# One written order of events per engine for the first layer of a two-layer decoder trunk

## The chip, the cores and the metric

The kernel runs on one core of a Trainium2 chip. The metric is device time in microseconds (us) of one execution, as the median of several. TensorE is called PE in the profile (its weight loads PEld), VectorE DVE, ScalarE ACT, GpSimd POOL, SyncE SP.

## The reference

Input x is 1024 tokens by 1024 channels, float32. Two layers are computed; after each, `x = LayerNorm(4^0.25 * x + mixer(x))`.

Layer 0 is a gated DeltaNet with 8 heads of width 128. A projection gives q, k, v and a gate z (32 column tiles of 128) and two small gate rows; q, k and v pass a causal convolution of 4 taps and SiLU; q and k are normalised. Per head and per chunk of tokens: decay and score matrices, a unit lower triangular inverse, and then a recurrence over the chunks:

```
v_new = u_n - w_n @ state
o     = q_n @ state + qk_n @ v_new
state = state * exp(gl_n) + kd_n.T @ v_new
```

The output of each head is RMS-normalised, multiplied by SiLU(z), and projected. Layer 1 is sliding-window attention; nothing of it is touched here.

## The kernel before

**Numbers and tiles.** Every float32 operand of a large product is split in a high and a low part, and a product is three matmuls (high-high, high-low, low-high) of 128 x 128 x 512. A projection group `g` is one column tile (128 channels) times one half of the tokens (512): 8 depth slices x 3 = 24 matmuls, `project` at L654. There are 64 groups after two for the gate rows: 6 for each head (q, q, k, k, v, v; heads 0 to 7), then 16 for z. One phase is six groups, 144 matmuls. Chunks of 128 tokens are used, so each head has 8.

**What hangs on a group.** After the last matmul of a group ACT copies the PSUM bank out (`evacuate`, L1099 and L1100), DVE does three taps of the convolution (`piece` 0 to 2, L1401), ACT a tanh (`gate_tanh`, L1106), DVE the last product (`piece` 3, L1418). The groups alternate between two PSUM banks. Weights of the next tile are fetched by DMA on ACT's queue and split on ACT (`high`, L1047) and DVE (`low`, L1325).

**What hangs on a head.** In this order:
- T, `token_major`: twice, 4 chunks at a time, PE transposes k, v and q of the head into banks 7, 5, 6 (L723); ACT copies v (L1113), DVE makes `k_dec` (L1483), ACT squares and sums k and q (L1122), each square waiting for the sum before it.
- M, `scores` on PE (L738, L739) for 8 chunks, with ACT's `exp` of the decay (L1190) and DVE's `matrices` (L1441, L1443), in banks 5, 6, 7 in turn.
- The inverse of the 32 x 32 diagonal blocks: SP sends the blocks out to HBM and back in another layout (L501, L506), POOL does 30 steps of two instructions (L609, L612), SP sends them back into `xT` (L509, L516). There is one `xT`, so SP waits for the last solve of the head before.
- X and L: DVE transposes blocks (L1513 to L1516), then four levels of small matmuls (`level`, L760 to L773) with copies on ACT and DVE between them complete the inverse of each chunk.
- Scan: for each chunk A (`with_state`, L784, L787), B (`solve`, L799) and C (`update`, L807, L809) on PE. Between A and B lies DVE's `resid` (L1531), between B and C ACT's `v_new` (L1208), between C and the next A DVE's `state` (L1540) and output sum (L1547); ACT scales `q_state` (L1203) and squares the output (L1129). A waits for the state and for the output sum of the chunk before.
- Output: OF, OS, OT: root of the sums, scaling (L1497), transposes back (`transpose_out`, L817) and copies into `tok` (L1184).

**What sets the order.** PE, ACT and DVE execute their instructions in program order. The order is written out by `plan(p, lag)`: for each phase `p` it gives every event a place, counted in matmuls from the start of the phase (constants `AT_...`, as a share of the phase), adds a lag per kind for ACT and DVE (`LAG_SCALAR`, `LAG_VECTOR`), and sorts. The lists of the phases are then run one after another, so all pieces of the last group of a phase stand ahead of everything of the next phase. Phases 8 and 9 have 10 and 6 groups (z), phase 10 has none: it holds the output of head 7 beside the first two steps of the output projection (`out_pair`, L826). SP and POOL have fixed orders of their own.

Of the kernel before, what the change touches and what calls it, by code (L numbers as in the profile page):

```python
# [100 lines left out]
def plan(p, lag):


    if p < GH:
# [1 line left out]
    elif p == GH:
        groups = list(range(QKV_GROUPS, QKV_GROUPS + GATE_SPLIT))
    elif p == GH + 1:
        groups = list(range(QKV_GROUPS + GATE_SPLIT, 2 * TILES))
    else:  # L110
        groups = []
    last = 2 * TILES - 2
    events = []
    for i, g in enumerate(groups):
        t0 = GROUP * i
        for q in range(0, GROUP, STEP):
            events.append((t0 + q, 0, ("mm", g, q)))
        end = t0 + GROUP - 0.5
        events.append((end, 1, ("end", g, 0)))
        if g % 2 == 0 and g // 2 + 1 < TILES:  # L120
            events.append((t0 + 6.6, 1, ("weights", g // 2 + 1, 0)))
            if g // 2 + 2 < TILES:
                events.append((t0 + 15.9, 1, ("fetch", g // 2 + 2, 0)))
        if g % 2 == 0 and g // 2 + 1 < TILES:
            events.append((t0 + 6.8, 1, ("low", g // 2 + 1, 0)))
        for k in range(CONV_K if g < QKV_GROUPS else 2):
            if g < last:
                events.append((end + 0.58 + k * 6.95, 2, ("piece", g, k)))
            elif k == 0:
                events.append((end + 0.2, 2, ("piece", g, k)))  # L130
    span = GROUP * max(len(groups), 1)
    slots = []
    if 0 <= p - 3 < GH or 0 <= p - 2 < GH:
        slots += [(AT_ROOTS, ("OF", 0))]
    if 0 <= p - 3 < GH:
        slots += [(AT_SCALE, ("OS", 0)), (AT_OUT, ("OT", 0))]
    if p == GH + 2:
        slots += [(0.02 + 0.02 * k, ("W", k)) for k in range(2)]
        for k in range(3, EARLY[0]):
            slots += [(0.14 + 0.02 * k, ("WW", k)), (0.145 + 0.02 * k, ("WO", k))]  # L140
    if p == GH + 1:
        events += [(t0 + 5.0 + 3 * k, 3, ("WO", k, 0)) for k in range(3)]
        events += [(t0 - 16.0 + 9 * k, 3, ("WW", k, 0)) for k in range(3)]
    if 0 <= p - 2 < GH:
        slots += [(AT_VALUES, ("VS", 0))]
    if 0 <= p - 1 < GH:
        slots += [(AT_TOKEN[i], ("T", i)) for i in range(2)]
        slots += [(AT_MATRIX + AT_MATRIX_STEP * c, ("M", c)) for c in range(NT + 1)]
    for r in (p - 3, p - 2):
        if 0 <= r < GH:  # L150
            blocks, inverse, scan, step = (AT_BLOCKS, AT_INVERSE, AT_SCAN, AT_SCAN_STEP) if r < GH - 1 else \
                                          (LAST_BLOCKS, LAST_INVERSE, LAST_SCAN, LAST_SCAN_STEP)
# [1627 lines left out]
```

## Time and profile before

| what | us |
|---|---|
| median of 3 runs | 1170.51 |
| the three runs | 1169.4, 1170.51, 2981.0 |
| the profiled execution | 1165.01 |
| its span, first to last instruction | 1163.0 |
| PE busy in it | 1067.3 (92%) |
| DVE, ACT, POOL busy | 720.4, 502.8, 322.1 |
| mean granted TensorE clock | 0.973 |

An instruction is shown with its line in the kernel before. "Busy" is the union of instruction times; matmuls overlap, so a busy PE can still hold short gaps. First group of layer 0's projection after the start-up: about 67 us; its last matmul starts at 652.71 us. The output projection follows, and from about 880 us layer 1's attention.

### The profile page before, as it was taken

What the parts mean: (1) busy time and instruction counts of PE and PEld (TensorE: products, weight loads), DVE (VectorE), ACT (ScalarE), POOL (GpSimd) and SP (SyncE); (2) the same over time, 40 slices, a digit from 0 to 9 for tenths busy, and PEclk for the clock granted to TensorE, in tenths of its full rate; (3) what the DMA queues carried; (4) which work ended last, traced back from release to release, by engine and by line L of the source; (5) the groups of instructions that cost most, each with busy time, mean ns of one, the idle gap of its engine ahead of it and who ended that gap; (6) DMA issues with size and microseconds to landing.
All of it is one profiled execution on the core that took longest, in us unless ns stands there. A gap on an engine that the chain in (4) does not pass through costs nothing. (4 is left out here: it accounts for less than half of the span.)

```text
span 1163.0 us, 17699 instructions
## 1 busy us (share of the span) xinstructions
PE 1067.3 (92%) x6325; PEld 847.9 (73%) x6325; DVE 720.4 (62%) x1650; ACT 502.8 (43%) x1386; POOL 322.1 (28%) x517
## 2 busy tenths in 40 slices
PE   7989678888979899898999999999997999999996
PEld 6768556666767676666877788888885777777885
DVE  4557446566556566664545877763437787787865
ACT  4453625546464554645343701120215656657100
POOL 1005857192855829393560000000000000000000
PEclk9999869999989999999999999999999999999998
DMA  5112111102012011201121241220200000012211
GB/s 185 56 37 64 37 37 46 46 21 62 28 28 64 24 50 38 55 19 46 47 61 40 91 145 45 65 82 1 64 19 1 28 29 20 19 49 94 94 55 55
DMA packets 74510, 59.50 MB, mean 51 GB/s; under 512 B 23148, under 2 KB 65196, under 8 KB 74424
## 3 DMA queue, kind: packets, MB, share of 16 engines
q1 hardware_dynamic: 40104, 41.53, 11.6%
q10 hardware_dynamic: 34320, 16.84, 5.6%
q8 instruction: 51, 0.84, 0.3%
q14 instruction: 35, 0.29, 0.1%
HBM read 52.04 MB, written 6.32 MB: 50 GB/s over the span
## 5 line engine op out<-in xcount | busy, mean ns | idle before, releaser
L654 PE MATMUL ps<-act_hi,w_hi 128*128 128x512 f32 x528 | 238.8, 452 | 0.0
L654 PE MATMUL ps<-act_hi,w_lo 128*128 128x512 f32 x528 | 211.6, 401 | 0.0
L654 PE MATMUL ps<-act_lo,w_hi 128*128 128x512 f32 x528 | 210.2, 398 | 0.0
L609 POOL TENSOR_TENSOR rank<-tok 32x30 f32<-32x30 f32 (+14 forms) x240 | 153.1, 638 | 48.6 <-DMA tok<-blocks_in 30.4
L612 POOL TENSOR_TENSOR tok<-tok,rank 32x30 f32<-32x30 f32 (+14 forms) x240 | 151.1, 629 | 18.8
L1401 DVE SCALAR_TENSOR_TENSOR tok<-xs,convw,tok 128x512 f32<-128x512 f32 x144 | 118.6, 824 | 32.3 <-ACT xs L1100 30.6
L654 PEld LDWEIGHTS ps<-act_hi,w_lo 128*128 128x128 f32 x528 | 101.4, 192 | 23.3
L654 PEld LDWEIGHTS ps<-act_hi,w_hi 128*128 128x128 f32 x528 | 102.9, 195 | 11.1
L654 PEld LDWEIGHTS ps<-act_lo,w_hi 128*128 128x128 f32 x528 | 103.0, 195 | 9.5
L826 PE MATMUL ps<-wo_hi,act_hi 128*128 128x512 f32 x256 | 100.5, 393 | 0.2 <-DVE wo_lo L1459 0.2
L826 PE MATMUL ps<-wo_hi,act_lo 128*128 128x512 f32 x256 | 99.7, 390 | 0.0
L826 PE MATMUL ps<-wo_lo,act_hi 128*128 128x512 f32 x256 | 99.6, 389 | 0.0
L597 POOL TENSOR_SCALAR_AFFINE_SELECT decay<-decay 128x1024 f32<-128x1024 f32 x8 | 8.7, 1094 | 217.5 <-DMA decay<-gc_rows 217.5
L1235 ACT ACTIVATE mv<-mv 128x1 f32<-128x1 f32 x16 | 3.2, 203 | 130.5 <-DVE mv L1608 130.5
L1203 ACT ACTIVATE q_state<-ps,sc_exp 128x128 f32<-128x128 f32 x56 | 20.6, 368 | 88.2 <-PE ps L787 88.1
L826 PEld LDWEIGHTS ps<-wo_hi,act_hi 128*128 128x128 f32 x256 | 48.1, 188 | 11.0 <-issue 1.0
L826 PEld LDWEIGHTS ps<-wo_hi,act_lo 128*128 128x128 f32 x256 | 48.0, 188 | 10.2
L826 PEld LDWEIGHTS ps<-wo_lo,act_hi 128*128 128x128 f32 x256 | 48.1, 188 | 9.8
L1325 DVE TENSOR_TENSOR w_lo<-w_raw,w_hi 128x1024 fp32r<-128x1024 f32 x33 | 43.6, 1322 | 15.2 <-ACT w_hi L1047 14.9
L981 PE MATMUL ps<-act_hi,z_hi 128*128 128x512 f32 x128 | 52.1, 407 | 0.1
L1106 ACT ACTIVATE th<-tok 128x512 f32<-128x512 f32 x48 | 30.1, 627 | 50.9 <-DVE tok L1401 50.8
L981 PE MATMUL ps<-act_lo,z_hi 128*128 128x512 f32 x128 | 51.7, 404 | 0.0
(235 smaller groups left out, 2292.4 us busy)
## 6 DMA issues: line engine op xcount, KB each, us to landing
w_raw<-in_a_w_in ACTq DMA_DIRECT2D x32, 512.0 KB, 4.2
tok<-in_x SPq DMA_DIRECT2D x8, 512.0 KB, 7.2
decay<-gc_rows SPq DMA_DIRECT2D x8, 512.0 KB, 4.3
xres<-in_x SPq DMA_DIRECT2D x8, 512.0 KB, 3.7
ws_raw<-in_b_w_in SPq DMA_DIRECT2D x16, 256.0 KB, 2.7
z_raw<-in_b_w_in SPq DMA_DIRECT2D x8, 512.0 KB, 3.8
out<-yr SPq DMA_DIRECT2D x8, 512.0 KB, 2.6
wo_raw<-in_a_w_out SPq DMA_DIRECT2D x6, 512.0 KB, 4.2
```

What stands on the lines that cost most here:

```text
L597: pool.affine_select(out=decay[:, :, :], in_=decay[:, :, :], compare_op=ALU.is_ge, fill=NEG, base=0, pattern=[[0, NT], [1, P]], channel_mu ...
L609: inner.next(pool.tensor_tensor(part, blocks[:, 0:m, m:m + 1].broadcast_to([32, m, w]), blocks[:, m:m + 1, m + 1:32].broadcast_to([32, m, ...
L612: inner.next(pool.tensor_tensor(blocks[:, 0:m, m + 1:32], blocks[:, 0:m, m + 1:32], part, ALU.add))
L654: mm = pe.matmul(ps[:, g % 2, :], lhs[:, k, :], rhs[:, k, HALF * b:HALF * (b + 1)], start=(i == 0), stop=(i == GROUP - 1))
L826: mm = pe.matmul(ps[:, OUT_BANKS[t] + half, :], lhs[:, k, t * P:(t + 1) * P], rhs[:, HALF * half:HALF * (half + 1)], start=(k == 0 and j = ...
L981: mm = pe.matmul(ps[:, GATE_BANK, :], lhs[:, k, :], rhs[:, k, HALF * b:HALF * (b + 1)], start=(i == 0), stop=(i == GROUP - 1))
L1106: act.activation(th[:, :], conv[g % 2], ACT.Tanh).then_inc(s_th, 1)
L1203: act.activation(q_state[:, :], ps[:, 3, 0:P], ACT.Copy, scale=sc["exp"][:, r, a:a + 1])\
L1235: act.activation(mv[:, t % 2, 3:4], mv[:, t % 2, 2:3], ACT.Sqrt).then_inc(s["sqrt"], 1)
L1325: dve.tensor_tensor(w_lo[w % 2][:, :, :], w_raw[:, :, :], w_hi[w % 2][:, :, :].bitcast(F32), ALU.subtract).then_inc(s_wlo, 1)
L1401: ins = dve.scalar_tensor_tensor(conv[b], xs[:, b, k:k + HALF], convw[:, k, tile:tile + 1], conv[b], ALU.mult, ALU.add)
```

## The change

It replaces the per-phase lists by one list per engine over the whole layer.

- `plan(at, lag)` makes one sorted list for each of PE, ACT and DVE. Every event of head h stands at `SPAN * (h + place + late)`, with SPAN = 144 matmuls. Places are tables of their own per engine (`AT_PE`, `AT_ACT`, `AT_DVE`), and each head has a shift for its first half (`LATE_TURN`: T, M) and for its second (`LATE_SCAN`: X, L, scan, output). From its first transposes to its output a head takes some 2.7 phases, from its first group 3.3.
- T is split in three: TQ (q, place 0.60, banks 7 and 5), TK (k, 0.95, banks 6 and 7) and TV (v, 1.27, banks 6 and 7, after the scores). The squares are written over their own PSUM source and don't wait for each other. The eight `exp` of a head's decay are one block on ACT (D).
- PSUM: `resid`'s product stays in bank 2, `q_state`'s goes to bank 4, B and C's output to bank 3, levels to 5 and 6, output transposes to 7 and 5. A no longer waits for the output sum.
- Two `xT` buffers: SP waits for the solves of the head before the last. `xr` and `uT` get room outside `o_tok`.
- In ACT's scan the copies QS, VN and the squares SO are placed one by one; in DVE's RE, ST, OA.
- `EARLY` goes from (5, 1) to (3, 1): the splits of output weights 3 and 4 are no longer written into the plan, and the output of head 7 comes before the end of the projection. The output projection then begins at k = 0 in `out_stage`.

The counts of matmuls, transposes, copies and DMAs stay; POOL clears four more slices at the start.

```
+SPAN = 6 * GROUP
+AT_PE = {"TQ": [0.6028], "TK": [0.9491],
+          "M": [0.9757, 0.9963, 1.017, 1.037, 1.058, 1.078, 1.099, 1.119],
+          "TV": [1.274], "OT": [3.261], "L": [2.332, 2.351, 2.388, 2.409],
+          "S": [2.415, 2.437, 2.458, 2.482, ...
+AT_DVE = {... "X": [2.276], "M": [0.9901, ..., 1.134], ...
+LATE_TURN = [-0.0781, 0.0, 0.1933, 0.15, 0.15, 0.1097, 0.0501, 0.05]
+LATE_SCAN = [0.204, 0.15, 0.15, 0.1, 0.0576, 0.05, 0.0, 0.1466]
+LAG_ACT = {"end": -0.528, "piece": 6.271, "weights": 0.867, "fetch": -0.08}
+LAG_DVE = {"piece": 2.595, "low": 4.624}
-    if p < GH:
-        groups = list(range(6 * p, 6 * p + 6))
...
+    for g in range(2 * TILES):
+        t0 = GROUP * g
...
+    for h in range(-1, GH):
+        for kind, places in at.items():
+            for i, place in enumerate(places):
...
+                late = 0.0 if kind == "TQ" else LATE_TURN[h] if kind in TURN_KINDS else LATE_SCAN[max(h, 0)]
+                name, c = STEPS[i] if kind == "S" else (kind, i)
+                events.append((SPAN * (h + place + late), 3, (name, h, c)))
     events.sort(key=lambda e: (e[0] + lag.get(e[2][0], 0.0), e[1]))
...
-                if h:
-                    sp.wait_ge(s_y, NT * h)
+                if h >= 2:
+                    sp.wait_ge(s_y, NT * (h - 1))
...
             def scores(h, c):
                 if c == 0:
-                    pe.wait_ge(s_tev, 2 * h + 2)
-                    pe.wait_ge(s_sk, NT * (h + 1))
+                    pe.wait_ge(s_sq, NT * (h + 1))
+                elif c == 1:
+                    pe.wait_ge(s_kd, 2 * h + 1)
+                    pe.wait_ge(s_sk, NT * h + 4)
+                elif c == 2:
+                    pe.wait_ge(s_kd, 2 * h + 2)
+                    pe.wait_ge(s_sk, NT * (h + 1))
...
                 pe.wait_ge(s_state, 7 * h + c)
-                pe.wait_ge(s_o, NT * h + c)
                 pe.matmul(ps[:, 2, 0:P], kT[h % 3][:, cut], state[:, :], start=True, stop=True).then_inc(s_ks, 1)
-                if 7 * h + c - 1 > 0:
-                    pe.wait_ge(s_oq, 7 * h + c - 1)
-                pe.matmul(ps[:, 3, 0:P], qT[h % 3][:, cut], state[:, :], start=True, stop=True).then_inc(s_qs, 1)
+                pe.matmul(ps[:, 4, P:2 * P], qT[h % 3][:, cut], state[:, :], start=True, stop=True).then_inc(s_qs, 1)
...
-            for p, events in enumerate(PLANS):
-                for kind, a, b in events:
+            for kind, a, b in PE_PLAN:
...
+            def sums(h, bank, out_sum, ready, done):
+                for i in range(2):
+                    act.wait_ge(ready, 2 * h + i + 1)
+                    for c in range(4 * i, 4 * i + 4):
+                        cut = ps[:, bank[i], (c - 4 * i) * P:(c - 4 * i + 1) * P]
+                        act.activation(cut, cut, ACT.Square, accum_out=sc[out_sum][:, h, c:c + 1]).then_inc(done, 1)
```

## Rows read from the trace of the kernel before

**Rows 1.** The page: each engine's busy time, granted clock in 40 slices.

```profile
PE 1067.3 (92%) x6325; PEld 847.9 (73%) x6325; DVE 720.4 (62%) x1650; ACT 502.8 (43%) x1386; POOL 322.1 (28%) x517
...
PEclk9999869999989999999999999999999999999998
```

**Rows 2.** By stretch: its us; busy PE, PEld, DVE, ACT, POOL; clock; DMA share, GB/s.

```profile
67.00:118.80 51.80, 47.71 (x243) 39.45 (x241) 31.72 (x56) 26.75 (x72) 18.62 (x25) 1.00 0.20 50
118.80:202.70 83.90, 64.13 (x396) 49.67 (x394) 44.33 (x89) 36.85 (x110) 60.92 (x100) 0.84 0.15 39
202.70:268.80 66.10, 58.02 (x396) 44.39 (x394) 40.54 (x86) 35.56 (x108) 38.00 (x58) 0.97 0.14 37
268.80:335.40 66.60, 58.80 (x395) 45.98 (x394) 41.80 (x86) 35.62 (x108) 40.09 (x63) 0.95 0.15 40
335.40:401.90 66.50, 59.35 (x396) 45.96 (x394) 40.73 (x86) 35.72 (x108) 40.17 (x63) 0.95 0.17 41
...
468.10:538.30 70.20, 62.37 (x423) 48.24 (x421) 42.82 (x88) 37.57 (x108) 42.59 (x72) 1.00 0.17 41
538.30:652.90 114.60, 108.21 (x744) 85.39 (x743) 60.04 (x125) 48.45 (x139) 33.60 (x61) 1.00 0.19 52
```

**Rows 3.** PE's waits within 335.4 to 401.9 us (total us, times, longest).

```profile
PE ps L807 <- ACT v_new L1208: 2.3, 1, 2.3
PE ps L738 <- ACT sq_junk L1122: 1.8, 1, 1.8
PE ps L723 <- ACT sq_junk L1122: 1.4, 2, 1.0
PE ps L784 <- DVE o_tok L1547: 0.7, 2, 0.5
PE ps L770 <- DVE o_tok L1522: 0.5, 1, 0.5
PE ps L817 <- DVE o_tok L1497: 0.4, 1, 0.4
```

**Rows 4.** Two of PE's waits over the whole run.

```profile
PE ps L723 <- ACT sq_junk L1122: 15.8, 16, 4.2
...
PE ps L760 <- DVE o_tok L1516: 12.9, 5, 10.5
```

**Rows 5.** The timeline at the end of one phase (start, duration).

```profile
385.26 2.87 DVE L1401 SCALAR_TENSOR_TENSOR tok<-xs,convw,tok 128x512 f32<-128x512 f32 x3 [0.65 <-ACT xs L1100]
...
388.16 0.63 ACT L1106 ACTIVATE th<-tok 128x512 f32<-128x512 f32 x1 [2.39 <-DVE tok L1401]
...
389.10 0.49 PE L807 MATMUL ps<-v_new,k_dec 128*128 128x128 f32 x2 [2.32 <-ACT v_new L1208]
```

**Rows 6.** The timeline of the inverse of head 0, and the start of head 1's.

```profile
91.95 0.28 DVE L1443 TENSOR_TENSOR aT<-ps,decay 128x128 f32<-128x128 f32 x1
...
99.43 0.24 POOL L609 TENSOR_TENSOR rank<-tok 32x30 f32<-32x30 f32 x1
...
144.73 0.14 POOL L615 MEMSET tok<- 32x32 f32 x1
...
151.22 0.44 DVE L1516 STREAM_TRANSPOSE o_tok<-xT 32x256 f32<-32x256 f32 x1
...
156.24 0.24 POOL L609 TENSOR_TENSOR rank<-tok 32x30 f32<-32x30 f32 x1
```

**Rows 7.** Busy time during the inverses of heads 3 and 7, columns as in rows 2.

```profile
294.20:337.70 43.50, 38.76 (x213) 29.92 (x210) 26.98 (x46) 22.02 (x67) 38.87 (x60) 0.96 0.09 25
564.70:602.80 38.10, 37.70 (x218) 31.18 (x217) 16.43 (x33) 12.58 (x34) 33.44 (x60) 1.00 0.11 28
```

**Rows 8.** The timeline of two projection matmuls in a row.

```profile
652.02 0.40 PE L654 MATMUL ps<-act_hi,w_lo 128*128 128x512 f32 x1
...
652.25 0.40 PE L654 MATMUL ps<-act_hi,w_hi 128*128 128x512 f32 x1
```

**Rows 9.** ACT's squares in the groups by line: busy us, mean ns of one.

```profile
L1122 ACT ACTIVATE sq_junk<-ps 128x128 f32<-128x128 f32 x128 | 35.2, 277 | 9.3 <-DVE k_dec L1483 4.6
```

More of the change, by code:

```diff
@@ L93, in slices_before, with plan @@
     return range(WR, SLICES) if n == refill else ()
-LAG_SCALAR = {"WO": 1.5, "WW": 0.0, "OT": 2.0, "end": 1.7, "piece": 5.5, "A": 1.6, "B": 0.3, "M": 3.0, "T": 0.6, "L": 6.3}
-LAG_VECTOR = {"WO": 5.0, "WW": 4.0, "piece": 0.9, "A": 0.1, "C": 0, "M": 0.8, "T": 1.9, "L": 7.5}
-def plan(p, lag):
-    if p < GH:
-        groups = list(range(6 * p, 6 * p + 6))
[L106 to L112, printed above, removed]
+def plan(at, lag):
     events = []
-    for i, g in enumerate(groups):
-        t0 = GROUP * i
+    for g in range(2 * TILES):
+        t0 = GROUP * g
         for q in range(0, GROUP, STEP):
@@ L121, in plan @@
             events.append((t0 + 6.6, 1, ("weights", g // 2 + 1, 0)))
+            events.append((t0 + 6.8, 1, ("low", g // 2 + 1, 0)))
             if g // 2 + 2 < TILES:
                 events.append((t0 + 15.9, 1, ("fetch", g // 2 + 2, 0)))
-        if g % 2 == 0 and g // 2 + 1 < TILES:
-            events.append((t0 + 6.8, 1, ("low", g // 2 + 1, 0)))
         for k in range(CONV_K if g < QKV_GROUPS else 2):
[L127 to L152, printed above, removed]
-            items = [(blocks, ("X", 0))] + [(inverse + AT_INVERSE_STEP * i, ("L", i)) for i in range(4)]
-            items += [(scan + step * (3 * c + i), ("ABC"[i], c)) for c in range(NT) for i in range(3)]
-            shift = p - 2 - r
-            slots += [(at - shift, (n, c, r)) for at, (n, c) in items if 0 <= at - shift < 1]
@@ L157, in plan @@
-    for at, item in slots:
-        events.append((at * span, 3, (item + (0,))[:3]))
-    events.sort(key=lambda e: (e[0] + lag.get(e[2][0], 0.0), e[1]))
-    out = [e[2] for e in events]
-    if p == GH + 2:
-        out += [("piece", last, 1), ("piece", last + 1, 1)]
-    return out
-PLANS, SCALAR_PLANS, VECTOR_PLANS = ([plan(p, lag) for p in range(GH + 3)] for lag in ({}, LAG_SCALAR, LAG_VECTOR))
+            events.append((end + 0.58 + k * 6.95, 2, ("piece", g, k)))
+    total = 2 * TILES * GROUP
@@ L169 @@
+    events.sort(key=lambda e: (e[0] + lag.get(e[2][0], 0.0), e[1]))
+    return [e[2] for e in events]
+PE_PLAN, ACT_PLAN, DVE_PLAN = plan(AT_PE, {}), plan(AT_ACT, LAG_ACT), plan(AT_DVE, LAG_DVE)
 class Link:
@@ L808, in update @@
                       .then_inc(s_su, 1)
-                pe.matmul(ps[:, 2, P:2 * P], aT[h % 2][:, c, :], v_new[:, :], start=True, stop=True)\
+                pe.matmul(ps[:, 3, P:2 * P], aT[h % 2][:, c, :], v_new[:, :], start=True, stop=True)\
                   .then_inc(s_av, 1)
@@ L913, in out_stage @@
                 before = (None, None, None, 0, 1, 3, 4, 5)
-                for k in range((2, 0)[i], NK):
+                for k in range(NK):
                     out_pair(i, k)
```

495 lines of the change are left out of this document (256 added, 239 removed), and 20 rows, old and new, of tables (AT_ACT, AT_DVE).

## The prediction

> **What bounds the kernel now.** I read the page first. PE is busy 92% of the span, and no other compute engine is above 62% [rows 1]. So the end is set by PE's stream, and time can only come out of it in two ways: fewer matmuls, which this change doesn't bring, or fewer gaps. The slices show where the clock is below its full 2.4 GHz: all but one or two of the lower digits lie in the first half, in layer 0 [rows 1].
>
> Then the busy times by stretch, cut from one head's transposes to the next's [rows 2]. Four stretches between 202.7 and 468.1 us are alike (66.1, 66.6, 66.5 and 66.2 us; the last is not shown). In the third PE is busy 59.35 of 66.50 us, 7.15 idle, at a mean clock of 0.95. A mean of 0.95 between the two levels 1.0 and 0.5 is a tenth of the stretch at 1.2 GHz, 6.6 us; work in it takes twice as long, so at most 3.3 us are lost, and I take half of that, 1.7, since idle time falls in these pieces too. The stretch 118.8 to 202.7 is the bad one: 19.8 us idle, clock 0.84, so 27 us at 1.2 GHz; without the idle 10.5 us some 16 us of work, half of it lost: 8 us. Before it, 4.1 us idle; after 468.1, 7.8 and then 6.4 [rows 2]. Together from 67 to 652.9 us: idle 4.1 + 19.8 + 8.1 + 7.8 + 7.2 + 7.3 + 7.8 + 6.4 = 68.5 us (7.3 is the stretch not shown), clock 8 + 4 x 1.7 = 15. That 83 us is all a new order could give.
>
> Third, what PE waits for in an ordinary stretch [rows 3]: 2.3 for `v_new`, 1.8 and 1.4 for the squares of k and q, 0.7 for the output sum, 0.5 and 0.4 for levels and output scaling. The list sums to 7.1, which is the idle time.
>
> **The change part by part.** The matmuls, transposes and copies stay the same in number, so each term is a wait.
>
> *The phase boundary, 2.3 us.* The row on the timeline is telling: DVE runs three taps in one go, 385.26 to 388.13, ACT's tanh waits 2.39 for them, and `v_new` stands behind the tanh, so PE waits 2.32 [rows 5]. These taps belong to the last group of a phase, and only because the lists are run phase by phase do they stand ahead of the remaining scan steps. One list per engine puts one tap between two scan steps. The wait goes to 0; taps and tanh are late next; they have 20 matmuls of 0.23 us [rows 8], 4.6 us, for 2.87 + 0.63 us of work.
>
> *Transposes and scores, 3.2 us (1.8 + 1.4).* Now k, v and q go through the banks twice, and PE waits each time until ACT has squared both k and q, 8 squares at 277 ns [rows 9] and their reads; q's now come 0.35 phase earlier, v's after the scores. What is left between TK and the third score is one set of eight squares of k, against two score pairs and 9 to 12 matmuls (some 3 us). But the eight `exp` are a block on ACT, behind it comes the tanh, and DVE's `piece` 3 waits for that ahead of the third pair of matrices, which frees the bank of the sixth score. I bound what remains by 0 and by today's 3.2, and take the middle, 1.6: gain 1.6.
>
> *Own banks, 0.7 us.* A waits for the state alone. DVE's output sum is the instruction behind it, so I take 0.5, between 0 and 0.7.
>
> *Levels and output scaling, 0.9 us.* Level 2 gets 5.4 instead of 2.8 matmuls of distance, OT stands 14 matmuls behind OS. Gain 0.7, between 0 and 0.9.
>
> *Clock, 1.7 us.* The low pieces follow the waits of 2 us and more; with the largest gone I take all of the 1.7, between 0 and 3.3.
>
> An ordinary stretch thus gives 2.3 + 1.6 + 0.5 + 0.7 + 1.7 = 6.8 us, and 66.5 becomes about 59.7. Five of them, 202.7 to 538.3: 34 us.
>
> *Head 0 and 1.* PE waits 10.5 us for head 0's inverse, and up to 4.2 for one set of transposes [rows 4]. Head 0's last score moves from place 1 + 0.2837 + 7 x 0.0233 = 1.447 to 1.119 - 0.078 = 1.041, 58 matmuls or 13.4 us earlier, while its X stays at 2.48 (2 + 0.4843; now 2.276 + 0.204). So the 10.5 go. Of the rest of that stretch (9.3 idle, 8 clock) I take 2.3 for its boundary, 4 at the transposes and all of the clock: 10.5 + 2.3 + 4 + 8 = 25. The stretch before: 2 of its 4.1. The last, 538.3 to 652.9: 2 of 6.4, since it has only one head's scores.
>
> *`EARLY`.* The end of the projection loses the output of head 7 from its edge, but the splits of weights 3 and 4 come later. ACT and DVE are free there; PE has three steps of 12 matmuls (2.8 us each) in hand. I take a loss of 1, between 0 and 3.
>
> *What an order by table costs.* Several hundred events get new neighbours in three queues. No row prices an order that hasn't run. The nearest are the small waits of the present order, 0.5 + 0.4 = 0.9 us a head [rows 3]; I take nearly twice that in each of 8 heads, 13 us, between 0 and 30 (half of the 7.1 of [rows 3], 8 times).
>
> Sum: 34 + 25 + 2 + 2 - 1 - 13 = 49 us. The profiled execution took 1165.0 us, so 1116; the median of the runs stands 5.5 us above it, and I carry that over: 1170.5 - 49 = 1121.
>
> **Does the inverse allow it?** Head 0's chain took 59.0 us from the last matrices (92.23) to the last block transpose, 45.3 of them on POOL; and POOL began the next 11.5 us after it ended [rows 6]. In an ordinary stretch the inverse takes 43.5 [rows 7], so POOL can turn a head around in 55.0 us, below the 59.7 I forecast. The tables leave 1.05 to 1.10 phases (151 to 158 matmuls) between the last matrices and X for heads 2 to 6: at 59.7 us for 144 they are 62.6 to 65.5 us, 3.6 to 6.5 more than 59.0. The second `xT` takes the solves out of it.
>
> POOL is slower beside a busy DVE: 43.5 us with DVE at 26.98 / 43.5 = 62%, 38.1 with 43% [rows 7]. DVE's 41 us a stretch [rows 2] in 59.7 would be 69%, and the same slope (5.4 us for 19 points) gives 45.5 us, a turnaround of 57.0: still below.
>
> The Trainium skill, page "SBUF — State Buffer", section "Who interferes with whom", says that a DVE instruction with two SBUF inputs and a GpSimd instruction that reads SBUF take turns, the later one blocked for the whole instruction. By that rule the inverse lengthens as the taps crowd in, and it speaks against this change; the trace agrees in direction (38.1 against 43.5 us).
>
> **The rivals.**
>
> *POOL becomes the bound (chance 0.20).* If the inverse takes 50 to 54 us in the denser stretches, a head costs 61.5 to 65.5 us and X, which stands in DVE's one queue, holds up taps and state behind it. For: the slope above, and the longest inverse of 45.3. Against: 50 needs more than twice that slope. At 63.5 us a stretch gives 3 instead of 6.8: 19 less over five, and some of the start goes too (5), so a gain of 25: 1146, with 1136 to 1160 around it.
>
> *The whole wait list goes (0.12).* Transposes without waits, and no new ones: 49 + 13 + 5 x 1.6 = 70; 1100.
>
> *Scan steps miss each other (0.09), the slower side.* A, B and C stand three matmuls (0.7 us) and the small ones apart, and between them lies a hop through DVE or ACT. If a tap (1.0 us, a third of 2.87 [rows 5]) or a split of weights stands ahead of `resid`, `v_new` or `state` in most steps, each of the 56 steps with a state loses 1 us or more; at 0.9 us per step (50 us) the gain is gone, at 1.3 (73 us) the time is 1195. For: `v_new` shows today what one wrong neighbour costs, 2.3 us. Against: the scan's pitch, 10.1 matmuls against 10.3, hardly changes.
>
> *The order isn't what made PE wait (0.08).* If DVE simply arrives late whatever the list, the waits move: about 1162.
>
> **How the numbers follow.** The forecast, 1121, has 0.51, with its own range 1106 to 1136 from the bounds of its terms. A difference of 2% (23 us) is about what a measurement can tell here from none. Faster by more: all of the forecast (0.51) and the full gain (0.12), and of the POOL case the better half and a little of the rest: 0.75. Within 2%: the rest of the POOL case and most of the last: 0.16. Slower: 0.09. The range goes from 1098 to 1158; it leaves out about 0.05 below and 0.13 above.
>
> **What would show it.** In the profile after: PE waits for `v_new` of 2 us and more are gone at the ends of phases; no wait of PE on the first level of head 0 above 2 us; stretches of 144 matmuls with all parts take 58 to 61 us, at clock 0.97 or better; PE's last projection matmul starts near 603 us. The step on POOL is wrong if inverses last over 48 us, or if DVE's X waits for the `xT` DMA. The forecast is wrong if PE idles over 4 us per head in A, B and C together.

## The result, and the profile after

The changed kernel takes 1090.53 us (median of 4 runs, 1087.56 to 1097.81), the kernel before 1171.95 beside it (median of 4, 1170.51 without the run of 2981.0 us); the ratio, without that run, is 0.932, with a 95% interval of 0.926 to 0.938. Forecast were 1121 us and a range of 1098 to 1158: the sign was right, the size was not, and the time lies below the range. The profiled execution took 1097.81 us, against 1165.01.

The page of the kernel after: busy times, granted clock, and the taps of the convolution, whose last columns are DVE's idle time ahead of them and what ended it.

```profile
PE 1043.7 (95%) x6325; PEld 847.0 (77%) x6325; DVE 725.1 (66%) x1650; ACT 497.4 (45%) x1388; POOL 332.4 (30%) x521
...
PEclk9999979999999999989999999999999999999999
...
L1409 DVE SCALAR_TENSOR_TENSOR tok<-xs,convw,tok 128x512 f32<-128x512 f32 x144 | 121.9, 847 | 9.8 <-ACT xs L1109 8.3
```

The same work by DVE and ACT, and PE's 6325 matmuls in 67 us less span [rows 1]. In the row of the taps the idle time behind ACT's copy is 8.3 us. In the page before it is 30.6, and the prediction gave this row no price:

```profile
L1401 DVE SCALAR_TENSOR_TENSOR tok<-xs,convw,tok 128x512 f32<-128x512 f32 x144 | 118.6, 824 | 32.3 <-ACT xs L1100 30.6
```

Where the time came from, by phases of 144 projection matmuls (from the starts of the matmuls in the two traces). Of the kernel before, and then of the one after, phases 3 to 7, five ordinary ones in a row:

```profile
186.40:251.10 64.70, 56.74 (x398) 43.01 (x396) 40.22 (x86) 35.62 (x108) 31.90 (x54) 1.00 0.16 42
251.10:317.80 66.70, 58.97 (x397) 46.04 (x396) 41.14 (x86) 35.66 (x107) 40.18 (x63) 0.95 0.15 40
...
450.40:516.50 66.10, 57.90 (x398) 44.46 (x396) 41.96 (x86) 35.52 (x107) 42.16 (x66) 0.97 0.16 41
sum 330.10, PE 291.76 PEld 225.44 DVE 204.88 ACT 178.11 POOL 192.98; mean PE 58.35 PEld 45.09 DVE 40.98 ACT 35.62 POOL 38.60
```

```profile
172.80:230.90 58.10, 55.17 (x403) 45.25 (x403) 42.57 (x87) 35.72 (x112) 39.37 (x62) 1.00 0.19 47
...
341.80:400.40 58.60, 56.65 (x410) 45.83 (x409) 42.67 (x89) 35.28 (x113) 43.36 (x65) 1.00 0.18 46
...
sum 284.70, PE 274.97 PEld 224.76 DVE 209.97 ACT 175.53 POOL 203.82; mean PE 54.99 PEld 44.95 DVE 41.99 ACT 35.11 POOL 40.76
```

330.1 us became 284.7, 45.4 less. Idle time fell from 38.3 to 9.7 us (28.6), busy PE from 291.8 to 275.0 (16.8). About half of the 16.8 is the clock: before, the one phase of the five without a slow piece has PE busy 56.74 us, the one with a piece of 3.4 us at 1.2 GHz 57.90, those with two 58.97 to 59.19. That puts the clock's part at 291.8 - 5 x 56.74 = 8.1 us. The other 8.7 us are busy time at the full clock; matmul ends are modelled, and no run says what it was.

The whole projection, in us from the first matmul of phase 0 (at 30.8 before, not at the 67 given ahead; at 31.5 after) to the start of PE's last one:

| part | before | after | less | forecast |
|---|---|---|---|---|
| phases 0 to 2 (fill, inverse of head 0) | 155.6 | 141.3 | 14.3 | 27 |
| phases 3 to 7 | 330.1 | 284.7 | 45.4 | 34 |
| phases 8 to 10 and end | 136.1 | 129.6 | 6.5 | 2 - 1 |
| cost of the new order | | | none seen | -13 |

The last row but one is 12.4 in the control run's trace (a0 below, 123.7 us): there the X of head 6 comes almost in time, and the wait of 3.4 us below is 0.8. The last phases also hold 22 matmuls fewer (822 against 844), which now stand in phases 3 to 7. The rows of the table add up to 66 us in this trace and 72 in the control's.

PE's waits over the whole run (total us, times, longest), the first two and the fourth:

```profile
PE ps L767 <- DVE tok L1523: 8.5, 1, 8.5
PE ps L742 <- DVE aT L1451: 8.0, 13, 1.2
...
PE ps L767 <- DVE qT L1523: 3.4, 1, 3.4
```

The longest in phases 3 to 7, before (186.4 to 516.5 us) and after (172.8 to 457.5):

```profile
PE ps L807 <- ACT v_new L1208: 11.4, 5, 2.4
PE ps L738 <- ACT sq_junk L1122: 8.9, 5, 1.8
PE ps L723 <- ACT sq_junk L1122: 6.8, 10, 1.0
PE ps L784 <- DVE o_tok L1547: 3.5, 9, 0.7
```

```profile
PE ps L742 <- DVE aT L1451: 5.7, 9, 1.0
PE ps L772 <- ACT tok L1205: 1.1, 2, 0.6
```

All of them add up to 37.9 us before and 9.5 after; in the phase 341.8 to 400.4 it is 1.8 us, against 7.1 [rows 3]. `v_new`, the output sum and nearly all of the squares' waits are gone. What is left is at the scores, which wait for DVE's `matrices` (0.5 us in the whole run before), and the first level of head 0, 8.5 us where it was 10.5 [rows 4]. Its timeline (start, duration), behind POOL's end at 131.1:

```profile
138.55 0.27 DVE L1520 MEMSET tok<- 32x256 f32 x1 [7.75 <-DMA xT<-blocks_out]
...
140.08 1.07 PE L767 MATMUL ps<-tok,nT 32*32 32x32 f32 x32 [8.50 <-DVE tok L1523]
```

And the columns of the stretch that holds the end of that wait and the time behind it, then of the inverses of two ordinary heads (2 and 6) and of head 0:

```profile
135.60:152.70 17.10, 11.85 (x119) 9.03 (x120) 4.80 (x10) 3.66 (x19) 8.23 (x18) 0.50 0.21 55
201.40:244.30 42.90, 40.99 (x327) 34.28 (x327) 29.87 (x62) 26.77 (x94) 38.27 (x61) 1.00 0.14 36
425.90:470.90 45.00, 43.49 (x268) 35.30 (x267) 32.96 (x70) 28.16 (x94) 40.37 (x61) 1.00 0.14 36
82.30:130.90 48.60, 47.03 (x232) 38.48 (x231) 36.55 (x57) 26.24 (x74) 43.97 (x60) 1.00 0.14 33
```

From the last matrices of head 0 (73.29) DVE's last block transpose begins 66.3 us later (139.59), with POOL at work for 48.6 of them; before it was 59.0 and 45.3. PE waits 8.5 us, and the clock is at 1.2 GHz for the 17.1 us from the wait's middle on.

### The profile page after: what moved, and what is told of

Read it like the earlier page. It is cut to its first block and busy times, and to the rows that moved or that the text cites. A ratio compares the mean times of both kernels' runs of the same rounds, so it can differ in the third digit from the quotient of the medians.

```text
span 1096.1 us, 17741 instructions
## 1 busy us (share of the span) xinstructions
PE 1043.7 (95%) x6325; PEld 847.0 (77%) x6325; DVE 725.1 (66%) x1650; ACT 497.4 (45%) x1388; POOL 332.4 (30%) x521
## 5 line engine op out<-in xcount | busy, mean ns | idle before, releaser
L649 PE MATMUL ps<-act_hi,w_hi 128*128 128x512 f32 x528 | 234.2, 444 | 0.0
L649 PE MATMUL ps<-act_hi,w_lo 128*128 128x512 f32 x528 | 209.3, 396 | 0.0
L649 PE MATMUL ps<-act_lo,w_hi 128*128 128x512 f32 x528 | 208.0, 394 | 0.0
L607 POOL TENSOR_TENSOR tok<-tok,rank 32x30 f32<-32x30 f32 (+14 forms) x240 | 160.7, 670 | 18.8
L1409 DVE SCALAR_TENSOR_TENSOR tok<-xs,convw,tok 128x512 f32<-128x512 f32 x144 | 121.9, 847 | 9.8 <-ACT xs L1109 8.3
L990 PE MATMUL ps<-act_hi,z_lo 128*128 128x512 f32 x128 | 51.9, 405 | 0.0
L896 PE MATMUL ps<-ws_hi,act_hi 128*128 128x512 f32 x128 | 51.7, 404 | 0.0
L1333 DVE TENSOR_TENSOR w_lo<-w_raw,w_hi 128x1024 fp32r<-128x1024 f32 x33 | 44.9, 1361 | 10.1 <-ACT w_hi L1056 10.0
```

What stands on the lines that cost most here:

```text
L607: inner.next(pool.tensor_tensor(blocks[:, 0:m, m + 1:32], blocks[:, 0:m, m + 1:32], part, ALU.add))
L649: mm = pe.matmul(ps[:, g % 2, :], lhs[:, k, :], rhs[:, k, HALF * b:HALF * (b + 1)], start=(i == 0), stop=(i == GROUP - 1))
L896: mm = pe.matmul(ps[:, TOKEN_BANKS[n % 4], 0:w], lhs[:, k, t * P:(t + 1) * P], rhs, start=(k == 0 and j == 0), stop=(k == NK - 1 and j == ...
L990: mm = pe.matmul(ps[:, GATE_BANK, :], lhs[:, k, :], rhs[:, k, HALF * b:HALF * (b + 1)], start=(i == 0), stop=(i == GROUP - 1))
L1333: dve.tensor_tensor(w_lo[w % 2][:, :, :], w_raw[:, :, :], w_hi[w % 2][:, :, :].bitcast(F32), ALU.subtract).then_inc(s_wlo, 1)
L1409: ins = dve.scalar_tensor_tensor(conv[b], xs[:, b, k:k + HALF], convw[:, k, tile:tile + 1], conv[b], ALU.mult, ALU.add)
```

## Experiments

**Reading them.** Ratios are to the kernel before on the same chip, with a 95% interval. Medians of the kernel before were 1164 to 1168 us on these chips. "Costs" compares the ratio with 0.936, the mean of the changed kernel and its two equals (a0, b1, b2), times 1166 us; with intervals of 0.003 to 0.005 a cost is known to some 5 us. A cost holds whatever the edit did to the clock as well.

**a0, the changed kernel again.** No edit but a comment.

> The changed kernel once more, beside the others on one chip, as the mark that they are read against. Both theories: about 1090 us (1087 to 1098), projection of layer 0 ended near 587 us, PE waits 8.5 us for head 0's inverse and some 17 us at 1.2 GHz follow.

Measured: 1090.4 us, ratio 0.9353 (0.9315 to 0.9391). So the gain is 75 us.

**a1, the kernel before with one list per engine.** Old places, old lags; phases 0 to 9 sorted together.

```diff
-    events.sort(key=lambda e: (e[0] + lag.get(e[2][0], 0.0), e[1]))
+    start = 6 * GROUP * min(p, GH) + (GROUP * GATE_SPLIT if p > GH else 0)
+    out = [(start + e[0] + lag.get(e[2][0], 0.0), e[1], p, e[2]) for e in events]
...
+    for p in range(GH + 2):
+        out += plan(p, lag)
+    out.sort(key=lambda e: e[:2])
```

> The kernel before, its places and lags kept, but the events of phases 0 to 9 sorted in one list per engine instead of phase by phase. Theory (the lists' seams made the wait for v_new): the 2.3 us wait at each of 7 seams goes, and with it one 3.4 us piece at 1.2 GHz each (1.7 us or more), so 28 us less than before: 1143 us. Rival (DVE is late whatever the list): 1165 to 1175 us, PE's wait for v_new still 2 us a head.

Measured: 1165.44 us, ratio 0.9996 (0.9972 to 1.0019): nothing. The step on the boundary was right in what goes and earned nothing: of the 13.3 us that PE waited for `v_new`, 0.2 are left, and the transposes of the output, 2.4 us before, are at the head of the list.

```profile
PE ps L827 <- DVE o_tok L1507: 16.1, 6, 3.3
```

The timeline shows whose turn it became:

```profile
325.14 1.28 ACT L1187 ACT_TABLE_LOAD   x1
...
326.76 1.28 ACT L1116 ACT_TABLE_LOAD   x1
328.05 0.63 ACT L1116 ACTIVATE th<-tok 128x512 f32<-128x512 f32 x1
...
328.71 0.72 DVE L1428 SCALAR_TENSOR_TENSOR vT<-th,tok 128x512 f32<-128x512 f32 x1 [3.33 <-ACT th L1116]
...
329.58 1.26 DVE L1507 TENSOR_TENSOR o_tok<-o_tok,sc_aq 128x1024 f32<-128x1024 f32 x1
...
330.90 1.09 PE L827 MATMUL ps<-ident,o_tok 128*128 128x128 f32 x8 [3.11 <-DVE o_tok L1507]
```

In the merged order `piece` 3 stands on DVE ahead of the output's scaling. It waits 3.33 us for the tanh, which stands on ACT behind the output's root and two function loads (1.28 us each); the scaling waits behind it, though ACT's root that it needs ended at 326.64, and PE behind the scaling. One head-of-line stop went, the next took its place.

**a2, the changed kernel with seams.** In all three lists the events of a phase's last group stand ahead of the next phase again.

```diff
-    events.sort(key=lambda e: (e[0] + lag.get(e[2][0], 0.0), e[1]))
+    def phase(e):
+        return min(e[2][1] // 6 if e[2][0] in ("piece", "end") else int(e[0] // SPAN), GH)
+    events.sort(key=lambda e: (phase(e), e[0] + lag.get(e[2][0], 0.0), e[1]))
```

> The changed kernel with the seams put back on all engines: pieces and evacuations of a phase's last group stand ahead of everything of the next phase. Theory: 2.3 us of wait and 1.7 us or more of clock return at 7 seams, 28 us: 1118 us. Rival (the new places leave room at the seam, so that it is not the list but the places that gained): under 8 us more, 1090 to 1098 us.

Measured: 1113.91 us, ratio 0.9552 (0.9508 to 0.9596): the seams cost 22 us here, where their removal from the kernel before gave none.

**a3, work for PE in the two long waits.** 36 matmuls of 128 x 512 whose product is not used stand ahead of the first level of head 0, 14 ahead of head 6's.

```diff
-                    pe.wait_ge(s_xr, h + 1)
...
+                    for _ in range({0: 36, 6: 14}.get(h, 0)):
+                        pe.matmul(ps[:, 5, :], act_hi[:, 0, 0:P], act_hi[:, 0, 0:HALF], start=True, stop=True)
+                    pe.wait_ge(s_xr, h + 1)
```

> The changed kernel with 36 matmuls of no use (128 x 128 x 512, into bank 5, which is free there) ahead of head 0's first level, where PE waits 8.5 us, and 14 ahead of head 6's, where it waits 3.4. Theory (the wait brings the clock down and the 17 us at 1.2 GHz after it cost as much as half of themselves): the wait stays as long in time, but the low stretch goes, 8 us less than the changed kernel: 1082 us. Rival (the low clock has another cause, or the work behind the wait is bound by the inverses anyway): 1088 to 1094 us.

Measured: 1095.98 us, ratio 0.9403 (0.9356 to 0.9449), 5 us more or none. The stretch of the wait, and one in phase 4, further on:

```profile
130.80:140.10 9.30, 9.30 (x71) 7.45 (x69) 2.80 (x6) 1.21 (x4) 0.00 (x0) 1.00 0.57 158
253.20:263.40 10.20, 10.20 (x48) 7.89 (x49) 4.05 (x6) 1.04 (x3) 7.95 (x16) 0.50 0.06 18
```

With PE kept busy the clock stays at 2.4 GHz in phase 2, which takes 58.9 us instead of 64.6. But 10.2 us at 1.2 GHz appear at 253.2, where PE had been busy 18.0 of the 20 us before without a wait over 1.1 us, and phase 4 takes 60.0 us instead of 54.8: what one gave, the other took. So the slow clock did follow the wait at 135, and the wait is not the only thing that it can follow.

**b1, A waits for the output sum again; b2, one `xT`'s order.** Two waits put back (the banks and the two buffers stay) whose removal the prediction had priced (0.5 a stretch) or relied on.

```diff
+                pe.wait_ge(s_o, NT * h + c)
```

```diff
-                if h >= 2:
-                    sp.wait_ge(s_y, NT * (h - 1))
+                if h >= 1:
+                    sp.wait_ge(s_y, NT * h)
```

> The changed kernel, but A of the scan waits for the output sum of the chunk before again, as the shared bank forced it to. Theory (a term of 0.5 to 0.7 us a head): 4 to 6 us more than the changed kernel, 1095 us. Rival (the sum is the next DVE instruction after the state, hidden by PE's three matmuls): under 2 us.

> The changed kernel, but SP waits for the solves of the head before, h - 1, ahead of filling the buffer, as with a single one. Theory (by the trace the last solve of head h - 1 is done before POOL ends head h's inverse): 0 to 2 us more. Rival (the second buffer is what lets the inverse run early): 5 us or more a head, 1125 us and above.

Measured: b1 1090.5 us, ratio 0.9371 (0.9338 to 0.9403); b2 1090.27, 0.9358 (0.9327 to 0.9389). Neither wait does anything in the new order.

**b3, q's transposes back beside k's.** TQ at 0.949, moved with its head.

```diff
-AT_PE = {"TQ": [0.6028],
+AT_PE = {"TQ": [0.9490],
...
-AT_ACT = {"TQ": [0.6242],
+AT_ACT = {"TQ": [0.9599],
...
-                late = 0.0 if kind == "TQ" else LATE_TURN[h] if kind in TURN_KINDS else LATE_SCAN[max(h, 0)]
+                late = LATE_TURN[h] if kind in TURN_KINDS or kind == "TQ" else LATE_SCAN[max(h, 0)]
```

> The changed kernel, but q is transposed and squared right ahead of k (TQ at 0.949 instead of 0.603, moving with the head), v stays behind the scores. Theory (both sets of squares between transposes and scores made the wait): 2 to 3 us a head more, with some clock: 1110 us. Rival (only the detour of v and the banks mattered): under 5 us.

Measured: 1103.06 us, ratio 0.9462 (0.9424 to 0.9499): costs 12 us. A wait like that of the kernel before (15.8 us) is back, at PE's transposes for ACT's squares; q's and k's sets share bank 7 here:

```profile
PE ps L724 <- ACT ps L1122: 11.1, 8, 2.0
```

**b4, the old lags.** All else as changed.

```diff
-LAG_ACT = {"end": -0.528, "piece": 6.271, "weights": 0.867, "fetch": -0.08}
-LAG_DVE = {"piece": 2.595, "low": 4.624}
+LAG_ACT = {"end": 1.7, "piece": 5.5}
+LAG_DVE = {"piece": 0.9}
```

> The changed kernel with the lags of the kernel before for evacuation and pieces (ACT end 1.7, piece 5.5; DVE piece 0.9) and none for the weights. Theory (each named wait is a matter of places; the lags only spare DVE short waits for the evacuation): up to 8 us more, 1098 us. Rival (the fit of neighbours in the queues is what carried the part of the gain that the terms don't explain): 20 us or more, 1110 us and above.

Measured: 1136.31 us, ratio 0.9759 (0.9725 to 0.9793): 46 us, the largest part that was undone by itself. DVE's idle time behind ACT's copy, of this kernel and then of the changed one (L1333: the low parts of the weights):

```profile
DVE tok L1409 <- ACT xs L1109: 37.5, 34, 3.0
```

```profile
DVE w_lo L1333 <- ACT w_hi L1056: 10.0, 5, 7.6
...
DVE tok L1409 <- ACT xs L1109: 8.3, 15, 1.8
```

PE's list in b4 begins so:

```profile
PE ps L742 <- DVE aT L1451: 20.0, 14, 3.1
PE ps L790 <- DVE state L1547: 14.4, 16, 1.7
```

With the old lags a tap stands on DVE 1.7 matmuls closer to the end of its group, and ACT's copy 2.2 later, so DVE stops in front of the tap. What stands behind it is late, as the timeline of one such stop shows:

```profile
249.29 1.28 ACT L1187 ACT_TABLE_LOAD   x1
...
251.99 0.75 DVE L1409 SCALAR_TENSOR_TENSOR tok<-xs,convw,tok 128x512 f32<-128x512 f32 x1 [2.95 <-ACT xs L1109]
...
252.92 0.28 DVE L1451 TENSOR_TENSOR aT<-ps,decay 128x128 f32<-128x128 f32 x1
...
253.25 0.78 PE L742 MATMUL ps<-kT 128*128 128x128 f32 x2 [2.75 <-DVE aT L1451]
```

ACT's copy comes behind a function load and two roots; DVE stops 2.95 us ahead of the tap, the matrices stand behind the tap, and PE waits 2.75 for them. What the stop costs is not DVE's time, of which there is enough, but that of whoever waits for the next instruction in DVE's queue.

**c1, the new lags in the kernel before; c2, with one list too.** c1 is the changed kernel's lags for `end`, `piece` and the weights in the old tables; c2 is c1 and a1 together.

```diff
-LAG_SCALAR = {"WO": 1.5, "WW": 0.0, "OT": 2.0, "end": 1.7, "piece": 5.5, "A": 1.6, "B": 0.3, "M": 3.0, "T": 0.6, "L": 6.3}
-LAG_VECTOR = {"WO": 5.0, "WW": 4.0, "piece": 0.9, "A": 0.1, "C": 0, "M": 0.8, "T": 1.9, "L": 7.5}
+LAG_SCALAR = {"WO": 1.5, "WW": 0.0, "OT": 2.0, "end": -0.528, "piece": 6.271, "weights": 0.867, "fetch": -0.08, "A": 1.6, "B": 0.3, "M": 3.0, "T": 0.6, "L": 6.3}
+LAG_VECTOR = {"WO": 5.0, "WW": 4.0, "piece": 2.595, "low": 4.624, "A": 0.1, "C": 0, "M": 0.8, "T": 1.9, "L": 7.5}
```

> The kernel before, phase by phase as it was, with only the lags of the changed kernel for evacuation, pieces and weights (ACT end -0.528, piece 6.271, weights 0.867, fetch -0.08; DVE piece 2.595, low 4.624). Theory A (DVE stands 30.6 us ahead of evacuations that aren't there yet, and all behind it is late; the lags end that): DVE's wait for L1100 falls under 12 us and the time by 15 to 30 us, 1135 to 1150. Theory B (lags and places only work as a fitted pair): within 8 us of the kernel before.

> The kernel before with one list per engine and the new lags together. Theory A: the wait of the output transposes for the scaling, which took the place of the seam's wait with one list alone (3.1 us a head), came from a late DVE and falls too, so 30 to 45 us less than the kernel before, 1120 to 1135. Theory B (the places of OF, OS, OT make that wait): no more than with the lags alone.

Measured: c1 1166.52 us, ratio 0.9986 (0.9964 to 1.0008); c2 1146.93, 0.9821 (0.9791 to 0.985). List alone 0, lags alone 0, both 21 us. c1's longest waits are the old ones (`v_new` 13.5 us, squares 16.2 and 14.2), and of DVE's 30.6 us in front of the taps 25.2 are left: in the old order the lags do not even end the stops that they are meant for. c2's list has no `v_new` at its head, and 4.7 of the 16.1 us of a1 (here DVE stops 23.2 us for the taps):

```profile
PE ps L748 <- ACT sq_junk L1132: 16.8, 8, 4.3
...
PE ps L827 <- DVE o_tok L1507: 4.7, 6, 1.0
```

What is left there beside the wait for head 0's X is the squares' part (16.8 + 10.6 us of waits), which is not in the changed kernel with its three sets of transposes.

**c3 and c4, the two main lags one by one, and d2, the lags of the weights.** c3: DVE's taps back to 0.9. c4: ACT's copies back to 1.7. d2: `weights`, `fetch` and `low` to 0.

```diff
-LAG_DVE = {"piece": 2.595, "low": 4.624}
+LAG_DVE = {"piece": 0.9, "low": 4.624}
```

```diff
-LAG_ACT = {"end": -0.528, "piece": 6.271, "weights": 0.867, "fetch": -0.08}
+LAG_ACT = {"end": 1.7, "piece": 6.271, "weights": 0.867, "fetch": -0.08}
```

```diff
+LAG_ACT = {"end": -0.528, "piece": 6.271, }
+LAG_DVE = {"piece": 2.595}
```

> The changed kernel with one number put back: DVE's lag of the pieces 0.9 instead of 2.595, 1.7 matmuls (0.4 us) earlier. Theory A: each first tap waits for its evacuation on DVE again, that wait is above 20 us in all and the time rises by 10 us or more. Theory B (the lag of the evacuation on ACT, 2.2 matmuls, is what mattered): under 5 us.

> The changed kernel with ACT's lag of the evacuation put back alone, 1.7 instead of -0.528. Theory A (evacuation late against the first tap, by either side): DVE's wait for L1109 above 20 us, 10 us or more slower. Theory B for this one (ACT has the room, the evacuation is done at the same time anyway): under 5 us. With the run before it says which of the two lags carries the 46 us of the old lags together.

> The changed kernel without its lags for the weights (ACT weights 0.867 and fetch -0.08, DVE low 4.624 all 0): DVE's subtraction stands ahead of the copy on ACT that it needs. Theory (a split of 1.3 us ahead of its input holds DVE like the taps do): 10 to 22 us more, 1100 to 1112 us. Rival (the 46 us are evacuation and taps multiplied): under 5 us.

Measured: c3 1104.14 us, ratio 0.9454 (0.9427 to 0.9482); c4 1100.29, 0.9425 (0.9398 to 0.9451); d2 1102.18, 0.945 (0.941 to 0.949). They cost 11, 8 and 10 us, 29 together against the 46 of b4: the rest comes only with all of them (or with ACT's tanh, 6.271 to 5.5, which b4 alone puts back). Of c4's 8 us some 5 sit in phase 6, which holds 10.2 us at 1.2 GHz from 373.6 on. In DVE's waits c3 and then d2 show each its own place, 8.3 and 10.0 us in the changed kernel (c4 has 22.1 in c3's place):

```profile
DVE tok L1409 <- ACT xs L1109: 18.9, 22, 2.7
```

```profile
DVE w_lo L1333 <- ACT w_hi L1056: 22.6, 19, 7.6
```

**e2, further the same way.** If it only mattered that DVE doesn't wait, more would be better.

```diff
+LAG_ACT = {"end": -1.1, "piece": 6.271, "weights": 0.867, "fetch": -0.08}
+LAG_DVE = {"piece": 3.3, "low": 4.624}
```

> The changed kernel with the lags moved further the same way: evacuation on ACT at -1.1 instead of -0.528, first taps on DVE at 3.3 instead of 2.595. Theory (DVE's wait for the evacuation, 8.3 us now, falls to under 4, but taps come later against the tanh and the scores): 0 to 6 us more than the changed kernel. Rival (the more lag, the less blocking): 3 us or more less, 1087 us.

Measured: 1105.69 us, ratio 0.948 (0.9446 to 0.9514), 14 us slower than the changed kernel. It is no test of the stops: DVE's wait in front of the taps is 9.3 us, no less than 8.3. PE's waits barely show the 14 us (7.5 us at L742 for the matrices, 8.0 in the changed kernel; 3.2 at L772 for ACT's copies, 1.1). The clock does: phases 3 and 4 take 64.4 and 60.5 us, 58.1 and 55.4 in the control, and each holds 10.2 us at 1.2 GHz, from 206.0 and from 267.4 on; here the 20 us ahead of the first of the two, and that piece:

```profile
186.00:206.00 20.00, 16.97 (x165) 13.22 (x163) 16.00 (x38) 14.01 (x31) 4.22 (x10) 1.00 0.32 80
206.00:216.20 10.20, 10.20 (x61) 7.82 (x51) 3.75 (x7) 0.59 (x1) 9.02 (x16) 0.50 0.01 2
```

These two phases have 11.4 of the 14 us. So these lags are worse than those of the changed kernel, but by where the clock falls more than by what waits; why it falls there is open.

**d1, seams and old lags; e1, old lags, q with k, and squares that wait; d3, the squares' waits alone.** d1 is a2 and b4 together; e1 is b4, b3 and d3.

```diff
+                        if NT * h + c:
+                            act.wait_ge(done, NT * h + c)
```

> The changed kernel with the seams put back and the old lags for evacuation, pieces and weights. Theory (both feed the same waits behind late taps, so they overlap): 46 to 60 us above the changed kernel, 1136 to 1150 us. Rival (they add): 70 us, 1160 us.

> The changed kernel, each square of q and k again waiting for the sum before it. Theory (the read of the sum, 195 ns, follows each square on the same engine, so the wait adds some 40 ns a square, 16 a head): 2 to 5 us more. Rival (the squares are on the path of every head's scores): 8 us or more.

> The changed kernel with old lags, q transposed right ahead of k, and the squares' own waits, all at once; the single list stays. Theory (different waits, so they add: 46 + 12 + 8 = 66 us): 1156 us, nearly all of the gain. Rival (they overlap as seams and lags did): 1140 us, and then 25 us of the gain belong to places and banks alone.

Measured: d1 1141.73 us, ratio 0.9793 (0.9761 to 0.9824); d3 1098.28, 0.9412 (0.9381 to 0.9442); e1 1152.5, 0.9865 (0.9817 to 0.9914). d1 costs 50 us, not 22 + 46: seams and lags pay for the same waits. d3 costs 6, seen in `v_new` (2.9 us, none in the changed kernel) and in the wait that is 1.3 us there:

```profile
PE ps L742 <- ACT ps L1124: 4.4, 7, 1.9
```

ACT's squares start 400 ns apart in d3, as in the kernel before, and 283 ns apart in the changed kernel (medians): the wait adds 117 ns to each, not 40, or 1.9 us a head. e1 costs 59 of the 75 us, and its parts add up to 64. Its list has all three in it:

```profile
PE ps L742 <- DVE aT L1453: 21.9, 16, 3.1
...
PE ps L724 <- ACT ps L1124: 12.7, 8, 2.3
```

**d4, the block of `exp` later.** A try to beat the kernel: D a third of a matmul later, against the 8.0 us at L742.

```diff
-          "D": [0.9888],
+          "D": [0.9912],
```

> The changed kernel with the block of exponentials on ACT 0.35 matmul later (place 0.9912), which in some heads puts one tanh ahead of it. Theory (the last waits at the scores, 8.0 us, come from the tap that waits for this tanh on DVE): 2 to 5 us less, 1086 us. Rival (the exponentials themselves are what the matrices wait for): 0 to 5 us more.

Measured: 1092.91 us, ratio 0.937 (0.9344 to 0.9395): no change, and PE's wait is 7.7 us. The time alone would fit the rival as well; but DVE's matrices wait for the `exp` once, 0.5 us, in the changed kernel. So neither of the two is what these 8.0 us come from. No kernel tried beats the changed one.

## Why the prediction was wrong

The terms of the sum beside what the profile shows (1165.0 and 1097.8 us), in us less. The forecast's stretches are cut up to 22 us later than the phases:

| term | forecast | measured |
|---|---|---|
| phases 3 to 7: waits | 5 x 5.1 = 25.5 | 28.6 |
| phases 3 to 7: clock | 5 x 1.7 = 8.5 | 8.1 |
| phases 3 to 7: busy time at full clock | - | 8.7 |
| phases 0 to 2: wait for head 0's inverse | 10.5 | 2.0 |
| phases 0 to 2: other idle time | 8.3 | 8.1 |
| phases 0 to 2: clock (measured: all busy time) | 8 | 4.2 |
| the end, `EARLY` | 1 | 6.5 (control 12.4) |
| cost of an order by table | -13 | none seen |
| sum | 49 | 66 (control 72) |

**The step that failed: "What an order by table costs", 13 us.** It measured none. For an ordinary phase the forecast left 2.05 us of idle time and added 1.6 for new neighbours; there are 1.9 (9.7 over five), new neighbours included. Without this term the sum is 62 us and the forecast 1108, still 18 us too long. Of the rest, 8.7 us are busy time that no term named and 5 to 11 the end; head 0 took 8.5 the other way. And the forecast carried over the 5.5 us by which the median stood above the profiled run, while 13 runs of the kernel before, beside the control, have a median of 1166.1. The term's reason, that several hundred events get new neighbours, is not wrong: with the old lags the same tables cost 46 us more (b4), above its upper bound of 30, and in a1 one new neighbour costs 16.1 us. It was priced from small waits of the old order, apart from the lags that decide it.

**What the price hung on: the lags.** They stood in the diff, 1.7 to -0.528 for `end` and 0.9 to 2.595 for `piece`, and the prediction gave them no price and no sign. Their 46 us (b4) don't come on top of the terms above: they are waits that the tables would bring (matrices 20.0 us and `state` 14.4, before 0.5 and none) and that the lags keep away. The row of the taps, 30.6 us of DVE's idle time in 33 stops of up to 3.0, was the place to ask what is queued behind. But it could not be read as a price: in the old order the lags gain nothing and leave 25.2 of it (c1). The prediction counted only PE's own waits, and took each for what it named last; why the instruction named there was late, it didn't ask.

**Phase boundary, 2.3 us each.** Right in what disappears: no wait for `v_new` is left. Wrong as a term of its own: removed alone it gives nothing (a1), since the 3.33 us stop behind a tanh takes its place; in the changed kernel it's worth up to 22 us (a2), shared with the lags.

**Transposes and scores, 1.6 (0 to 3.2).** Near the middle: in the five phases the waits at L723 and L738 were 16.2 us (8.9 + 6.8 for the squares, 0.5 for the matrices) and are 7.1 at the same places (5.7 for the matrices, 0.7 for the squares, 0.7 for copies), 1.8 a phase. The prediction named the right remainder, the scores behind the matrices. Undone, q's place costs 12 us (b3) and the squares' waits 6 (d3), 18 or 2.3 a head.

**Own banks, 0.5 a stretch; second `xT`.** The waits for the output sum are gone, 0.7 a phase, but they are as good as gone when A asks for it again (1.0 us in the whole run of b1, 6.0 before): DVE's order does it. What the banks themselves are worth was not run. That the second `xT` "takes the solves out of it" was not needed either.

**Clock, 1.7 (0 to 3.3).** The size held: the mean clock is 1.00 in all five phases, and by the rows of the phases before with no, one and two slow pieces it is 8.1 us, 1.6 a phase. The reason was loose. Seven pieces of 3.4 us lie in these phases; four follow the waits of 2.3 and 2.4 us for `v_new`, but three begin with the wait of 1.8 us at the scores.

**Head 0 and 1, 25 + 2.** 14.3 us. This is the second step that failed, and it hid part of the first. The 10.5 us became 8.5, not 0. PE came to its first level 49.0 us after the last matrices before and 58.3 now, 9.3 later and not 13.4, and the chain beside it grew by 7.3; that leaves 2.0. The chain from the matrices to X grew from 59.0 to 66.3 us: 3.3 on POOL, 1.8 on the way out to HBM (9.0 us from the matrices to POOL's first step, 7.2 before [rows 6]) and some 2 on the way back. PE arrived sooner than forecast since the phases in between got shorter. The arithmetic in places, 1.041 to 2.48, was right, and was converted at the old pace. With the wait stayed its clock: 17.1 us at 1.2 GHz, 27.3 before. The kernel before had DVE waiting for the `xT` DMA here as well, 10.01 us, so for head 0 that mark of the prediction tells nothing of the change:

```profile
150.18 0.27 DVE L1513 MEMSET o_tok<- 32x256 f32 x1 [10.01 <-DMA xT<-blocks_out]
```

The transfers out and back run beside a busier DMA now, which may be why they take longer (not tested), in windows of the kernel before and then of the one after (next to last column: DMA share):

```profile
92.20:99.40 7.20, 7.20 (x34) 5.94 (x33) 3.58 (x6) 3.04 (x7) 1.03 (x1) 1.00 0.42 112
144.70:151.70 7.00, 0.00 (x0) 0.00 (x0) 1.46 (x5) 0.00 (x0) 0.14 (x1) 0.52 0.32 56
```

```profile
73.30:82.30 9.00, 9.00 (x46) 7.47 (x45) 6.67 (x9) 3.53 (x6) 1.13 (x2) 1.00 0.55 146
130.90:139.60 8.70, 0.68 (x4) 0.22 (x2) 1.02 (x4) 1.63 (x3) 0.15 (x1) 0.77 0.45 106
```

**`EARLY` and the end, +2 - 1.** 6.5 to 12.4 us. The last phases gained as well: PE idles 5.0 us in them, 1.9 in the control, against 8.8. How much of that is `EARLY` was not run.

**The inverse, and the POOL rival (0.20).** It did not become the bound, but it came closer than the argument had it. The inverses of heads 1 to 6 take 41.7 to 45.0 us, not 50; from the start of one to the start of the next are 55.1 to 57.2 from head 1 on, where the prediction had 57.0, and that is just what a phase takes. From head 5 on POOL and SP go round without a pause: the last matrices of heads 5, 6 and 7 are ready 2.0, 2.6 and 5.7 us before SP, still busy with the head before, can send them. For head 6 DVE's last block transpose begins 64.3 us after the last matrices, where the prediction took 59.0:

```profile
478.23 0.27 DVE L1520 MEMSET qT<- 32x256 f32 x1 [4.28 <-DMA xT<-blocks_out]
```

PE waits 3.4 us there, and 6.8 us at 1.2 GHz follow from 480.4 on. In the control the wait is 0.8, the clock stays, and phase 8 takes 54.5 us instead of 60.3. Both marks set for this step came up, an inverse over 48 us (head 0, 48.6) and X waiting for the `xT` DMA (heads 0 and 6). The Trainium skill, page "SBUF — State Buffer", section "Who interferes with whom", has a DVE instruction with two SBUF inputs and a GpSimd instruction that reads SBUF take turns; the trace agrees in direction, within the changed kernel: 38.9 us with DVE 45% busy, 41.7 with 60%, 42.9 with 70%, 45.0 with 73%, 48.6 with 75% (but 44.9 with 69%). The slope itself didn't carry over: the prediction had 45.5 at 69%, and 43.5 at 62% [rows 7] lies above 42.9 at 70%.

**The other rivals.** "The whole wait list goes" (0.12, 1100) came nearest and is still 9 us above. It, too, had the lags at nothing. "Scan steps miss each other" did not happen: PE waits for `state` once, 0.3 us, in the five phases. But b4 shows its mechanism, `state` late 16 times for 14.4 us; the new lags are what prevents it. "The order isn't what made PE wait" is refuted by b4 and e1, which keep every operation and give back 46 and 59 us.

**Open.** The 16 us between e1 and the whole gain: seams, banks and the places of the tables were not undone on top of it. The 8.7 us of busy time at full clock. And what the slow clock follows in the pieces of 10.2 us (a3, c4, e2).

**By the marks set beforehand.** PE's last projection matmul starts at 587.1, not near 603. Phases of 144 take 54.8 to 58.6 us at clock 1.00, at or below the 58 to 61. PE's whole idle time is 1.9 us a phase, under the 4 that would have refuted it. The first level of head 0 failed its mark, and so did the two of the inverse.

## What to carry to other kernels

In queues that run in order, price a change of order as a whole: one stop removed hands its time to the next instruction in line (list alone 0, lags alone 0, both 21 us; in the changed kernel 46 for the same lags). Read the idle rows of engines that aren't the bound too, and ask what stands behind the waiting instruction. The row's size is no price: 25.2 us of DVE in front of the taps went with no gain (c1), 23.2 with 21 us (c2). When a step is moved by a share of a phase, convert it at the new phase's length, and ask whether the chain beside it shrinks as well: here it grew. Look at the clock of every variant before reading its cost: in e2 most of it sat in two slow pieces.
